# A hybrid attention and recurrent layer on one core: first modulation factors in four column groups, all row squares taken ahead, and the border between sample attention and output projection overlapped

## The reference, cut to what matters

```python
def pre_mixer(x, c, lp):
    mods = jnp.split((jax.nn.silu(c) @ lp['w_ada'] + lp['b_ada'])[:, None, :], 6, axis=-1)
    h = rmsnorm(x, lp['ln1']) * (1.0 + mods[1]) + mods[0]
    return mods, split_proj(h @ lp['w_in'])

def post_mixer(x, mods, o_r, o_c, o_s, o_w, gates, lp):
    ...
    attn = g[:, :, 0] * o_c + g[:, :, 1] * o_s + g[:, :, 2] * o_w
    merged = jnp.concatenate([rmsnorm(o_r, lp['gn_rnn']),
                              rmsnorm(attn.reshape(B, S, ATTN_WIDTH), lp['gn_attn'])], axis=-1)
    x = x + mods[2] * (merged @ lp['w_out'])
    h = rmsnorm(x, lp['ln2']) * (1.0 + mods[4]) + mods[3]
    ff = (jax.nn.silu(h @ lp['w_gate']) * (h @ lp['w_up'])) @ lp['w_down']
    return x + mods[5] * ff
```

## Time and profile before

| what | value |
|---|---|
| three runs | 2071.31, 2073.29, 2079.03 us, median 2073.29 us |
| the profiled execution | 2076.35 us, its span 2074.6 us |
| TensorE busy | 1843.0 us, 89% of the span |
| VectorE, ScalarE, GpSimd busy | 919.0, 727.9, 268.7 us |
| mean granted TensorE clock | 0.927 of full speed |
| moved by DMA | 214.12 MB, 103 GB/s mean |

### The profile page before, as it was taken

One profiled execution on the slowest core, in us unless ns is written; L12 is line 12 of the kernel. 1 busy time (PEld: TensorE's weight loads), 2 busy tenths in 40 slices (PEclk: granted clock), 3 DMA queues, 4 the chain that ended last, 5 costly groups with the idle time before them and its releaser, 6 DMA issues. The chain is left out here.

```text
span 2074.6 us, 31385 instructions
## 1 busy us (share of the span) xinstructions
PE 1843.0 (89%) x11299; PEld 1635.5 (79%) x11299; DVE 919.0 (44%) x1694; ACT 727.9 (35%) x1194; POOL 268.7 (13%) x264
## 2 busy tenths in 40 slices
PE   8999797867997988987588699799999999999998
PEld 3899574425885877976365599799999999999998
DVE  2422574023446666664233455344434444344433
ACT  3310340112444554653111334453323533235322
POOL 1100001231100000000000043030240402400022
PEclk9999899987997988988798799899999999999999
DMA  7111562005430000002250345454454454554543
GB/s 260 37 46 30 147 182 88 0 27 188 160 106 5 2 0 0 0 1 108 110 205 1 101 130 176 131 138 129 122 154 131 132 149 131 153 138 126 149 134 98
DMA packets 313343, 214.12 MB, mean 103 GB/s; under 512 B 20509, under 2 KB 300621, under 8 KB 309998
## 3 DMA queue, kind: packets, MB, share of 16 engines
q1 hardware_dynamic: 306604, 172.34, 29.0%
q0 software_dynamic: 4816, 40.73, 5.1%
q10 hardware_dynamic: 1842, 0.05, 0.1%
HBM read 205.81 MB, written 11.41 MB: 105 GB/s over the span
## 5 line engine op out<-in xcount | busy, mean ns | idle before, releaser
L416 DVE TENSOR_TENSOR ff_lo<-ff_raw,ff_hi 128x2048 fp32r<-128x2048 f32 (+1 forms) x126 | 264.8, 2102 | 217.3 <-ACT ff_hi L412 217.3
L421 PE MATMUL banks<-low_rows,ff_hi 128*128 128x352 f32 x1120 | 360.4, 322 | 0.0
L420 PE MATMUL banks<-ff_h_hi,ff_hi 128*128 128x352 f32 x1056 | 342.9, 325 | 13.6 <-DVE ff_lo L416 13.3
L422 PE MATMUL banks<-ff_h_hi,ff_lo 128*128 128x352 f32 x1056 | 340.3, 322 | 0.0
L412 ACT ACTIVATE ff_hi<-ff_raw 128x2048 fp32r<-128x2048 f32 (+1 forms) x126 | 215.2, 1708 | 234.0 <-PE banks L422 233.8
L421 PEld LDWEIGHTS banks<-low_rows,ff_hi 128*128 128x128 f32 x1120 | 211.5, 189 | 0.3
L420 PEld LDWEIGHTS banks<-ff_h_hi,ff_hi 128*128 128x128 f32 x1056 | 199.0, 188 | 15.1 <-issue 14.9
L422 PEld LDWEIGHTS banks<-ff_h_hi,ff_lo 128*128 128x128 f32 x1056 | 199.6, 189 | 0.0
L420 PE MATMUL banks<-hid_hi,ff_hi 128*128 128x352 f32 x528 | 171.9, 326 | 4.3 <-DVE hid_lo L416 4.1
L422 PE MATMUL banks<-hid_hi,ff_lo 128*128 128x352 f32 x528 | 170.6, 323 | 0.0
L421 PE MATMUL banks<-hid_lo,ff_hi 128*128 128x352 f32 x528 | 170.1, 322 | 0.0
(11 more groups left out here) (377 smaller groups left out, 3221.5 us busy)
## 6 DMA issues: line engine op xcount, KB each, us to landing
ff_raw<-in_w_gate SPq DMA_DIRECT2D x66, 512.0 KB, 4.0
ff_raw<-in_w_up SPq DMA_DIRECT2D x66, 512.0 KB, 5.3
ff_raw<-in_w_down SPq DMA_DIRECT2D x48, 384.0 KB, 3.8
late_ada<-in_w_ada SPq DMA_DIRECT2D x32, 512.0 KB, 4.7
ff_raw<-in_w_down SPq DMA_DIRECT2D x48, 320.0 KB, 3.0
ff_raw<-in_w_out SPq DMA_DIRECT2D x24, 512.0 KB, 5.0
s_raw<-in_w_in SPq DMA_DIRECT2D x48, 128.0 KB, 2.4
streams<-in_x_prompt SPq DMA_DIRECT2D x4, 1024.0 KB, 9.0
```

Source lines behind the costliest of these rows:

```text
L416: return dve.tensor_tensor(lo, raw, hi.bitcast(F32), ALU.subtract)
L420: pe.matmul(out, lhsT=w_hi, rhs=x_hi, start=first, stop=False)
L421: pe.matmul(out, lhsT=w_hi, rhs=x_lo, start=False, stop=False)
L422: return pe.matmul(out, lhsT=w_lo, rhs=x_hi, start=False, stop=last)
```

## The change

Three places are edited, and the parts of each hang together.

1. In the first block the eight products of a piece go to four groups of 32 output partitions (`factor_quarters`): chunk c into partitions 32(c mod 4) on. `cT` is widened to 32 columns a chunk, filled up with zeros. VectorE copies 128 partitions, and `turn_quarters` multiplies by a 128 x 9 matrix `gather` (four identities below one another) that turns and adds the four parts. `factor_sums`, now on columns 0 to 8, stays for the later factors.
2. In `keys_and_values` GpSimd takes the squares of all three row groups first, the second and third into `q_tmp` once the queries are rotated, and then scales.
3. At the border: the eight prompt tiles of `attn` are squared and scaled at the head of `sample_attention`; the first `w_out` block is loaded there, into the place of `kTs`; the last group's way through DRAM is started in `trunk`, behind the load of the second block. In `trunk` no prompt tile is scaled, the recurrent halves are split by ScalarE and GpSimd (`z_part`), and TensorE starts each sum with the attention chunks (`CHUNKS`). The 32 sample rows are scaled later.

```diff
+def factor_quarters(pe, out, w, cT):
+    for c in range(KD):
+        q = slice(c % 4 * 32, c % 4 * 32 + 32)
+        m = pe.matmul(out[q, :], lhsT=cT[:, c, :], rhs=w[:, c, :], start=(c < 4), stop=(c >= KD - 4), skip_group_check=True)
+    return m
+def turn_quarters(pe, bank, at, parts, gather, n):
+    for m in range(n):
+        r = pe.matmul(bank[:, ds(at * COND + m * COND, COND)], lhsT=parts[:, m * P:(m + 1) * P], rhs=gather, start=True, stop=True)
+    return r
...
-                factor_sums(pe, ps[q][0:COND, :], w[q], cT).then_inc(mods_summed, 1)
+                factor_quarters(pe, ps[q], w[q], cT).then_inc(mods_summed, 1)
...
+            s.done(dve.memset(cT[:, :, :], 0.0))
+            dve.wait_ge(ident_loaded, 16)
+            s.then(dve.tensor_tensor(gather[:, :], ident[:, 0:COND], ident[:, 32:32 + COND], ALU.add))
...
-        z_sum = sb(nc, st, "z_sum", [P, GR])
+        z_sum = [sb(nc, st, "z_sum", [P, GR]), qtmp[:, 0, :], qtmp[:, 1, :]]
...
                 if g:
-                    pool.wait_ge(z_summed, g)
+                    pool.wait_ge(queries_rotated, 1)
...
                 pool.sem_inc(z_acc, 1)
+            for g in range(NG):
                 pool.wait_ge(z_rated, g + 1)
...
+            sp.dma_start(gain_row, bcast(d["gn_attn"][0], 0, P)).then_inc(gain_loaded, 16)
...
+                else:
+                    sp.wait_ge(k_used, SG * UN)
+                    for x in load_out(d, 0, first_raw):
+                        sp.dma_start(*x).then_inc(first_loaded, 16)
                 sp.wait_ge(out_taken, g + 1)
...
+                if g + 1 < SG:
+                    return_rows(sp, d, g, out, attn, out_stored, out_back)
...
-            sp.wait_ge(out_back, 16 * SG * BT * N_KV)
...
+            s = Steps(act, act_stepped)
+            for t in range(TILES):
+                if t == 4:
+                    s.fence()
+                s.done(act.activation(score_space[:, t % 4 * 512:(t % 4 + 1) * 512], attn[:, t, :], ACT.Square,
+                                      accum_out=attn_sum[:, t:t + 1]))
+            s.fence()
+            act.activation(attn_sum[:, :], attn_sum[:, :], ACT.Sqrt, bias=eps[:, 0:1], scale=1.0 / ATTN_WIDTH).then_inc(attn_rooted, 1)
...
+            for t in range(TILES):
+                s.done(dve.scalar_tensor_tensor(attn[:, t, :], attn[:, t, :], attn_sum[:, t:t + 1], gain_row, ALU.mult, ALU.mult))
...
-            for n in range(LEAD):
+            for n in range(1, LEAD):
...
+                if n == 1:
+                    sp.dma_start(gain_row, bcast(d["gn_attn"][0], 0, P)).then_inc(gain_loaded, 16)
+                    return_rows(sp, d, SG - 1, sample_out, attn, out_stored, out_back)
...
-                    for c in range(KD):
+                    for c in CHUNKS:
+                        if c == 0 and j == 0:
+                            pe.wait_ge(z_lo_done, g + 1)
...
-            act.wait_ge(stat_clear, 1)
-            square_tiles(0, 4)
-            square_tiles(4, T9)
-            part(order[0])
             hi(0, 2, 0, 2 * KD)
-            for p in order[1:6]:
+            for p in order[0:4]:
                 part(p)
+            z_part(0)
             hi(0, 2, 1, 2 * KD)
-            part(order[6])
+            part(order[4])
+            z_part(1)
...
+            z_part(2)
+            act.wait_ge(out_back, 16 * DEC_BATCH * N_KV)
+            act.activation(h_f[0:RS, 0:2, 0:ATTN_WIDTH // 2], attn[0:RS, TILES, :].rearrange("p (a n) -> p a n", a=2), ACT.Square, accum_out=rows_rstd[0:RS, :]).then_inc(attn_squared, 1)
...
-            scale_tiles(0, 4, 1)
-            part(order[0])
             lo(0, 2, 0, 2 * KD)
-            for p in order[1:6]:
+            for p in order[0:5]:
                 part(p)
-            scale_tiles(4, T9, 2)
             lo(0, 2, 1, 2 * KD)
...
+            def z_part(g):
+                pool.wait_ge(z_hi_done, g + 1)
+                pool.tensor_tensor(m_lo[g % 2][:, 0:KR, :], z_gate[:, :, rows_of(g)], m_hi[g % 2][:, 0:KR, :].bitcast(F32), ALU.subtract
+                                   ).then_inc(z_lo_done, 1)
+            z_part(0)
+            z_part(1)
+            pool.memset(acc_out[:, :], 0.0).then_inc(pad_clear, 1)
+            pool.wait_ge(out_back, 16 * DEC_BATCH * N_KV)
+            sum_squares(lambda c: xT[:, c, rows_of(0)], acc_mid[0], x_mid, 0, mid_acc)
+            z_part(2)
+            sum_squares(lambda c: xT[:, c, rows_of(1)], acc_mid[1], x_mid, KD, mid_acc)
```

More of the change, by code:

```diff
@@ L1837, in _ @@
             s = Steps(dve, stepped)
+            dve.wait_ge(attn_rooted, 1)
+            s.then(dve.reciprocal(attn_sum[:, :], attn_sum[:, :]))
+            dve.wait_ge(gain_loaded, 16)
+            for t in range(TILES):
+                s.done(dve.scalar_tensor_tensor(attn[:, t, :], attn[:, t, :], attn_sum[:, t:t + 1], gain_row, ALU.mult, ALU.mult))
+            s.fence()
             dve.wait_ge(masks_loaded, 64)
@@ L1915, in _ @@
                 dve.tensor_copy(out, ps[6][0:QR, :]).then_inc(out_taken, 1)
+    return first_base, first_raw, out
 OUT_BLOCKS = KD // 2
@@ L1927, with load_out @@
 YT = 3
+def load_out(d, n, w):
+    view = d["w_out"][0].rearrange("(k p) n -> p k n", p=P)
+    return [(w[:, j * KD:(j + 1) * KD, :], view[:, :, (n % OUT_BLOCKS * 2 + j) * P:(n % OUT_BLOCKS * 2 + j + 1) * P]) for j in range(2)]
 def rows_out(d, g, j):
@@ L1976, in tile_rows @@
         return min(P, ROWS - t * P)
-    order = [("z", 0, 0), ("t", 0, 0), ("t", 1, 0), ("t", 2, 0), ("t", 2, 1), ("t", 3, 1), ("z", 0, 1), ("t", 4, 1), ("t", 5, 1),
-             ("t", 5, 2), ("z", 0, 2), ("t", 6, 2), ("t", 7, 2), ("t", 8, 2)]
+    order = [(0, 0), (1, 0), (2, 0), (2, 1), (3, 1), (4, 1), (5, 1), (5, 2), (6, 2), (7, 2), (8, 2)]
     after = {part: n + 1 for n, part in enumerate(order)}
+    CHUNKS = list(range(KR, KD)) + list(range(KR))
     T_BANK = [4, 5, 6, 7, 4, 5, 7, 4, 5]
@@ L1985, in trunk @@
     with ExitStack() as st:
-        raw = [sb(nc, st, f"ff_raw{p}", [P, 2 * KD, P]) for p in range(2)]
+        raw = [first_raw, sb(nc, st, "ff_raw1", [P, 2 * KD, P])]
         w_hi = [sb(nc, st, f"ff_hi{p}", [P, 2 * KD, P], F32R) for p in range(2)]
@@ L1992, in trunk @@
         h_f = sb(nc, st, "h_rows", [P, KD, GR])
-        sq = [sb(nc, st, f"ff_sq{p}", [P, GR]) for p in range(2)]
+        sq = sb(nc, st, "ff_sq", [P, GR])
         acc_out = sb(nc, st, "acc_out", [P, YT * P])
@@ L2141, in _ @@
                 turn(t)
-            pe.wait_ge(m_lo_done, after[("t", 2, 0)])
+            pe.wait_ge(m_lo_done, after[(2, 0)])
             out(0)
@@ L2220, in _ @@
             s = Steps(act, act_stepped)
-            def square_tiles(a, b):
-                for t in range(a, b):
-                    n = tile_rows(t)
-                    if t - a >= 4:
-                        s.fence()
-                    s.done(act.activation(ps[t % 4][0:n, 0:ATTN_WIDTH], attn[0:n, t, :], ACT.Square, accum_out=stat[0:n, t:t + 1]))
-                s.fence()
-                act.activation(rows_rstd[:, a:b], stat[:, a:b], ACT.Sqrt, bias=eps[:, 0:1], scale=1.0 / ATTN_WIDTH
-                               ).then_inc(attn_rooted, 1)
             def hi(i, per, b, n):
@@ L2315, in _ @@
             hi(0, 2, 8, 2 * KD)
-            for p in order[11:]:
+            for p in order[8:]:
                 part(p)
@@ L2367, in _ @@
             s = Steps(dve, stepped)
-            def scale_tiles(a, b, n):
-                dve.wait_ge(attn_rooted, n)
-                s.then(dve.reciprocal(rows_rstd[:, a:b], rows_rstd[:, a:b]))
-                for t in range(a, b):
-                    n = tile_rows(t)
-                    dve.scalar_tensor_tensor(attn[0:n, t, :], attn[0:n, t, :], rows_rstd[0:n, t:t + 1], gain_row[0:n, :],
-                                             ALU.mult, ALU.mult).then_inc(attn_scaled, 1)
             def lo(i, per, b, n):
@@ L2473, in _ @@
             lo(0, 2, 3, 2 * KD)
-            part(order[7])
-            part(order[8])
+            part(order[5])
+            part(order[6])
             take(2)
@@ L2479, in _ @@
             lo(0, 2, 5, 2 * KD)
-            part(order[9])
-            part(order[10])
+            part(order[7])
             take(4)
             lo(0, 2, 6, 2 * KD)
+            dve.wait_ge(attn_rooted, 1)
+            s.then(dve.reciprocal(rows_rstd[0:RS, :], rows_rstd[0:RS, :]))
+            dve.wait_ge(gain_loaded, 16)
+            dve.scalar_tensor_tensor(attn[0:RS, TILES, :], attn[0:RS, TILES, :], rows_rstd[0:RS, :], gain_row[0:RS, :], ALU.mult, ALU.mult
+                                     ).then_inc(attn_scaled, 1)
             take(5)
@@ L2608, in _ @@
                     else:
-                        s.then(pool.tensor_tensor(sq[0][:, :], x, x, ALU.mult))
-                        r = pool.tensor_tensor(acc, acc, sq[0][:, :], ALU.add)
+                        s.then(pool.tensor_tensor(sq[:, :], x, x, ALU.mult))
+                        r = pool.tensor_tensor(acc, acc, sq[:, :], ALU.add)
```

165 lines of the change are left out of this document (85 added, 80 removed), and 2 rows, old and new, of the table start.

## The result

| | before | changed |
|---|---|---|
| median | 2074.61 us (4 runs, 2071.31 to 2079.03) | 2027.28 us (4 runs, 2023.83 to 2029.87) |
| ratio | | 0.9771, 95% interval 0.9756 to 0.9786 |
| profiled execution | 2076.35 us, span 2074.6 | 2023.83 us, span 2022.1 |
| TensorE busy | 1843.0 us | 1817.5 us |
| mean granted clock | 0.927 | 0.932 |

The changed kernel is 47 us faster; 46 were forecast. The table at the end of the experiments shows where such spread sits.

A forecast was written before the change was run, and what follows sets the result against it. TensorE, busy 89% of the span, was taken as the bound. Terms -6.4 - 23.9 - 16.4 + 0.7 = -46.0 us took the profiled 2076.35 to 2030.3, and 3.06 less for the median gave 2027 us; range 2018 to 2039.

The forecast's parts named there:

- nine steps of 3.96 us: First block's factor sums: only a chunk's second record runs beside the next one's first, 3.96 us a sum instead of 7.04.
- 1 us for the low clock: First block, last factor sum: TensorE stands still some 3 us before it, adding 1 us, between 0 and 3.5.
- Rival 1: First block: column groups do not run side by side; gain 0 or loss up to 7 us, 2033.7 to 2040; chance 0.17.
- rival 2: All four column groups run at once and TensorE keeps the full clock at the border; 2020.5 us; chance 0.13.
- theory A: Follow-up's theory, factor sums in pairs: a product waits for its own group, holding all behind; 8.8 us at low clock.
- One sign of being wrong: First block's end: the forecast is wrong if the projection starts later than 6 us after the bias.
- The regained clock: `keys_and_values`: slow work behind the two waits goes too, 1.7 + 1.9 + 1.5 us on top of 18.8.
- The block change: Border: from VectorE's last copy in the sample block to `trunk`, taken as 1.0 us.
- The low clock in `out(0)`: Border: TensorE still stands 3 to 4 us before `out(0)`, so its slow products stay; could fall by 3.0 us.
- The recurrent half: `out(0)`: GpSimd's subtraction done 8.4 us into the block, TensorE there at 9.7 or 8.0: hidden, or a 0.4 us wait.
- The gain row ahead of the window: Head of the sample block: the row adds 0.26 MB ahead of the window's transfer, +0.7 us.
- Rival 3: Feed-forward: the 12.7 us wait for a weight block goes (2011 us) or happens twice (2043 us); chance 0.05 each.

The follow-up runs named there:

- the run in pairs: The changed kernel with the eight chunks of a factor sum handed to the four column groups two by two instead of one after the other; one run, 2025.30 us.
- the doubled split: The changed kernel with GpSimd's subtraction of the recurrent half for row group 0 done twice; one run, 2030.65 us.

## Why the prediction was right, point by point

**Part 1: the size nearly right, the mechanism wrong.** Forecast -6.4, measured -8.1 in the trace and 7.9 us by undoing it. That TensorE was the bound and the last landing would take over at 42.3 us held. The step that failed is "both records of a product write the same columns, and records of one engine start in order", which made nine steps of 3.96 us. A timeline is listed by time of start, so it could not have shown another order. All groups in fact run at once, in both orders tried: 7.04, 3.63 and 1.92 us for one, two and four groups at the full clock. The second error stood beside it: 1 us for the low clock. The sum ran wholly at clock 0.50, which costs 3.60 - 1.92 = 1.7 us, because shorter sums leave TensorE standing ahead of each piece and not only the last. The forecast had 3.96 + 1 = 5.0 us where 3.6 were measured: one term was 2.0 us too high, the other 0.7 too low, and they partly cancelled, which is luck. Rival 1 falls; of rival 2 the first half held (four at once) and the second did not (the full clock).

The Trainium skill ("TensorE: Matmul & The Clock Gate", the part on packing small matmuls) measures 2.38 times for three column tiles. Here four gave 7.04 / 1.92 = 3.7 times at the same clock, so it pointed the right way where the forecast's rule did not. It also says that matmuls start strictly in program order; if a group takes one product at a time, that makes the 8.8 us of theory A, and the 3.67 us of the run in pairs do not agree with it.

One sign of being wrong came true and means nothing: the projection starts 6.69 us behind the bias (54.55 and 47.86 us), where the forecast allowed 6. Before the change it was 6.67 us (62.64 and 55.97), so the mark was set too low. The bias itself came at 47.86 us, not near 50.

**Part 2: right in size and mechanism.** Forecast -23.9, measured -24.1 in the trace and 23.9 us by undoing it. The regained clock was a real term: the waits alone would have left 5 us unexplained. The squares of groups 1 and 2 ran from 330.7 to 343.6 us, and TensorE asks for the first of them at 389.5. What the forecast left out is their neighbour: VectorE's 32 small copies beside them took 11.5 instead of 4.0 us (below). VectorE's first copy of a tile came some 6 us later against the shifted stage, still without a wait of TensorE.

**Part 3: right.** Forecast -16.4, measured -16.9. The block change took 0.42 us where 1.0 was taken. `out(0)` followed 6.2 us into the block (6.1 forecast). The low clock in `out(0)` stayed as forecast: 5.4 us for 18 products, against 5.2 for 17. The recurrent half was hidden as worked out, done at 8.2 us (8.4) with TensorE there at 9.9 (9.7); the margin, 1.7 us in this trace, is 1.6 by the doubled split. The third block's load went out at 11.5 us (about 10), and its high half came 8.2 us after ScalarE was free without holding TensorE.

**The gain row ahead of the window, +0.7: there, and rather larger.** From SP's first transfer of the block to the product on the window are 32.2 us in the changed kernel, against 31.5 before. All twelve traces with the row have 32.2 to 33.4 us, 32.9 in the mean; the two without it have 31.5 and 31.7. That is about 1.3 us. How much of it is the row and how much the squares and scalings that went to the same place, no run separates.

**The collision.** Rival 3 asked whether it would move; it stayed, 12.6 against 12.7 us. Its price was put at 12.7 + 3 us; cutting the copy into pieces gave 14.9.

**The sum.** The trace gives -8.1 - 24.1 - 16.9 = -49.1 us, or about -48 with the gain row; the ratio gives 47.5 with about 3 either way, and the forecast was 46.0. What it lacked is mostly part 1, 1.7 us short. That the median came out at 2027.28 us for a forecast of 2027 is closer than the terms were.

## What to carry to other kernels

A float32 sum over chunks with few output rows can be spread over the four groups of 32 output partitions, in either order tried here, and costs about a quarter. But then the loads can become the bound, and the work between the waits ran at the low clock: price the shorter work at the clock that its own new gaps leave. A wait costs its length plus the slow work behind it; with both taken from the rows, part 2 came out right to 0.2 us. One long DRAM to DRAM copy held up the weight loads of another queue at both places where it was put; in pieces of half a megabyte, 10.5 us apart, it caused no wait above 1 us.

## What the runs showed of the hardware that was not expected

- **Column groups of float32 products overlap, in rotation and in pairs alike**, with two records a product. Four records start together and the next four 0.85 us later at the low clock, 0.43 at the full one. A record is shown longer than such a step (about 1.06 us at the low clock), so durations of records do not add up to the time of a sum:

```profile
L220 PE MATMUL banks<-early_ada,cT x32: 1014/1061/1063, 34.1 to 44.9; 128*32 128x512 f32 x32
```

- **GpSimd's sums stretch VectorE's small copies.** VectorE's copies of 64 x 16 took 167 ns each before. While GpSimd's squares ran they took 466 and 332 ns, the longest 0.92 us, and GpSimd's own instructions kept their 0.77 and 0.93 us. Groups of VectorE in that stretch of the changed kernel (count, busy us, mean ns, idle before):

```profile
L1041 DVE COPY q_plain<-streams 64x16 f32<-64x16 f32 x16 | 6.8, 466 | 0.4
L1041 DVE COPY q_rot<-streams 64x16 f32<-64x16 f32 x16 | 4.7, 332 | 0.0
```

The Trainium skill ("SBUF — State Buffer", its list of terms, "shared port pair") has VectorE and GpSimd take a pair of ports in turn, the loser blocked for a whole instruction; the stretched copies agree with that, though which of the two was blocked each time no row shows.

- **A transfer instruction can itself stand.** SP's issue of one `w_up` block took 12.33 us while GpSimd's copy was under way; the other 65 of that line took 0.53 to 0.86. What it stood for, no row shows.
- **Idle products hold the clock.** With 24 of them the clock stayed at 1.00 from 32 to 44 us, where it was 0.50 without. The 8 ahead of `out(0)` kept it at the full level too, at no cost, since nothing else was ready to run.
